# Sample attention on one Trainium2 core: pages turned on VectorE, scores in 32-row tiles, values undivided ahead of the next scores

## The reference, cut to what matters

```python
def mla_attend(q_lat, q_pe, q_pos, c_kv, k_pe, k_pos, w_uv):
    s = (jnp.einsum('bthc,bsc->bhts', q_lat, c_kv) + jnp.einsum('bthr,bsr->bhts', q_pe, k_pe)).astype(jnp.float32) * MLA_SCALE
    s = jnp.where(k_pos[None, :] <= q_pos[:, None], s, -jnp.inf)
    p = jax.nn.softmax(s, axis=-1).astype(c_kv.dtype)
    o_lat = jnp.einsum('bhts,bsc->bthc', p, c_kv)
    return jnp.einsum('bthc,chv->bthv', o_lat, w_uv)
...
    past = cache_mla[i][page_table].reshape(db, n_pages * PAGE_SIZE, MLA_LAT)
```

## Time and profile before

| | |
|---|---|
| median of 3 runs (lowest, highest) | 1845.02 us (1843.95, 1851.87) |
| span of the profiled execution, first to last instruction | 1837.3 us |
| profiled execution's own time | not given apart; the span and what lies around it, 7.7 us if it is the median |
| PE / DVE / ACT / POOL busy | 94% / 35% / 19% / 2% of the span |
| mean granted TensorE clock | 0.976 |
| prompt's attention with the first pair's pages | 126.4 to 181.7 us of the span |
| samples' attention, four pairs | 181.7 to 322.7 us |

### The profile page before, as it was taken

One profiled execution on the slowest core, in us unless ns is written; L12 is line 12 of the kernel. 1 busy time (PEld: TensorE's weight loads), 2 busy tenths in 40 slices (PEclk: granted clock), 3 DMA queues, 4 the chain that ended last, 5 costly groups with the idle time before them and its releaser, 6 DMA issues.

```text
span 1837.3 us, 41974 instructions
## 1 busy us (share of the span) xinstructions
PE 1732.0 (94%) x19056; PEld 1137.2 (62%) x19056; DVE 640.1 (35%) x1196; ACT 345.0 (19%) x558; POOL 39.7 (2%) x49
## 2 busy tenths in 40 slices
PE   6989898789899999998999999999999999999994
PEld 6967565589899999996934435344353534447342
DVE  5534443674865544855632010120101002010021
ACT  3223231402443333534210000000000000000001
POOL 0010000000000000000000000000000000010100
PEclk9999999698999999999999999999999999999998
DMA  9130540200854443517499999999999999997995
GB/s 292 52 112 1 150 141 20 38 3 4 240 161 151 150 137 105 170 62 230 172 386 414 418 413 418 415 417 417 410 417 403 417 415 406 417 398 306 415 405 220
DMA packets 171303, 474.02 MB, mean 258 GB/s; under 512 B 28426, under 2 KB 114604, under 8 KB 140228
## 3 DMA queue, kind: packets, MB, share of 16 engines
q1 hardware_dynamic: 168574, 461.05, 66.3%
q0 software_dynamic: 2352, 10.23, 1.6%
q10 hardware_dynamic: 198, 0.05, 0.0%
HBM read 459.19 MB, written 15.24 MB: 258 GB/s over the span
## 4 chain that ended last, share of the span: by engine, by line
PE 47%; SPq 3%; DMA 2%; DVE 1%; issue 1%; ACT 0%; POOL 0%; POOLq 0%; ACTq 0%; DVEq 0%
PE bank L2662 43%; SPq L2321 2%; DMA ring<-in_moe_w_down 1%; PE bank L319 1%; PE bank L320 1%; PE bank L321 1%; SPq L2431 0%; SPq L2325 0%; PE bank L2513 0%; PE bank L2592 0%; PE bank L2636 0%; DMA ring<-y_rows_dram,y_index 0%; PE bank L2528 0%; PE bank L2547 0%; PE bank L2630 0%
## 5 line engine op out<-in xcount | busy, mean ns | idle before, releaser
L2662 PE MATMUL bank<-ring,x 128*32 128x512 f32 (+1 forms) x6144 | 587.3, 540 | 2.3 <-DMA ring<-in_moe_w_gu 2.0
L2662 PEld LDWEIGHTS bank<-ring,x 128*32 128x32 f32 x6144 | 203.9, 110 | 354.4 <-issue 333.7
L2662 PE MATMUL bank<-ring,hid 128*32 128x256 f32 x5376 | 292.1, 379 | 0.3 <-DMA ring<-in_moe_w_down 0.3
L2662 PEld LDWEIGHTS bank<-ring,hid 128*32 128x32 f32 x5376 | 184.4, 110 | 108.1 <-issue 2.3
L319 PE MATMUL bank<-x_hi,w_hi 128*128 128x320 f32 (+1 forms) x488 | 151.8, 311 | 0.0
L320 PE MATMUL bank<-x_lo,w_hi 128*128 128x320 f32 (+1 forms) x488 | 150.8, 309 | 0.0
L321 PE MATMUL bank<-x_hi,w_lo 128*128 128x320 f32 (+1 forms) x488 | 150.8, 309 | 0.0
L2130 DVE TENSOR_TENSOR w_lo<-ring,w_hi 128x2048 fp32r<-128x2048 f32 (+2 forms) x51 | 112.5, 2209 | 97.5 <-ACT w_hi L2052 97.2
L3015 DVE TENSOR_TENSOR hrow<-sil,bank 128x512 f32<-128x512 f32 (+1 forms) x48 | 26.9, 617 | 301.3 <-PE bank L2662 301.3
L2052 ACT ACTIVATE w_hi<-ring 128x2048 fp32r<-128x2048 f32 (+2 forms) x51 | 94.1, 1848 | 126.8 <-PE bank L321 124.2
L2787 ACT ACTIVATE sil<-bank 128x512 f32<-128x512 f32 (+1 forms) x48 | 22.7, 544 | 455.2 <-PE bank L2662 455.2
(11 more groups left out here) (576 smaller groups left out, 2122.8 us busy)
## 6 DMA issues: line engine op xcount, KB each, us to landing
ring<-in_moe_w_gu SPq DMA_DIRECT2D x128, 1024.0 KB
ring<-in_moe_w_down SPq DMA_DIRECT2D x112, 1024.0 KB
ring<-in_moe_w_gu SPq DMA_DIRECT2D x128, 768.0 KB
ring<-in_ffn_w_gu_even SPq DMA_DIRECT2D x44, 512.0 KB, 4.9
pages<-in_cache_mla SPq DMA_DIRECT2D x128, 144.0 KB, 2.5
ring<-in_w_in_odd SPq DMA_DIRECT2D x12, 1024.0 KB, 5.3
ring<-in_ffn_w_down_even SPq DMA_DIRECT2D x10, 1024.0 KB, 5.4
proj_ring<-in_w_in_even SPq DMA_DIRECT2D x9, 1024.0 KB
```

Source lines behind the costliest of these rows:

```text
L2662: mm = t.matmul(ps[banks[g3]][SL * y:SL * y + SL, 0:w], act[:, g3, k, :], m_ring[:, slot, at + y * w:at + (y + 1) * w], start=start, stop= ...
```

## The change

**Turning pages.** PE's transposes and the copies out of PSUM are gone. DVE turns a page in 32x32 blocks from SBUF to SBUF: ten instructions for a pair (`QUARTERS`, four pages of 256 columns for one sample each, and two of 512 columns for the rotated keys). In such a block layout the latent's 32 rows of a chunk lie in each of the four groups of 32 partitions, one group for each quarter of a page's positions.

**Scores.** Nine chunks of 32 rows in place of three. For each chunk there are eight products: rows group k (32 partitions) by sample x (64 columns), `tile_position=(32*k, 64*x)`, 512 keys each, group k into bank k. The queries must lie in all four groups of partitions: SyncE writes them to DRAM once and loads them back for each pair (`load_queries`, four DMAs).

**Order.** `scores(p+1)` follows directly on the values of pair p. The values stay undivided in bank 4 or 5 (`acc(p)`), ACT divides them on the way out. ACT does all copies of turned probabilities and values. `mix` moves from DVE to POOL. SP loads quads 0 and 1 once half of the values that used the buffer are through (`v_half`), then waits for the scores of the pair before (`s_full`) to load the queries, then for `v_full` for the other quads.

```diff
+                def load_queries(sp, pair):
+                    for g in range(4):
+                        sp.dma_start(qrep[32 * g:32 * g + 32, :, :], q_dram[:, :, 2 * NQ * pair:2 * NQ * (pair + 1)].rearrange("c r q -> r c q")).then_inc(q_in, 16)
...
-                NT = 20
...
+                QUARTERS = [(quad, x) for quad in range(4) for x in range(2)]
+                NT = len(QUARTERS) + 2
+                def turn(v, pair, rows, e):
+                    quad, x = QUARTERS[e] if e < len(QUARTERS) else (3, e - len(QUARTERS))
+                    v.wait_ge(page_in[(2 * pair + x) % 4][quad], 64 * (pair // 2 + 1))
+                    if e < len(QUARTERS):
+                        four = slice(4 * quad, 4 * quad + 4)
+                        return v.transpose(pgT[:, x, four, :], rows[:, x, four, 0:KVR])
+                    return v.transpose(pgR[:, x, :, :], rows[:, x, :, KVR:LAT])
...
+                                sp.wait_ge(q_low, 2)
+                                for c in range(2):
+                                    sp.dma_start(q_dram[4 * c:4 * c + 4].rearrange("c r q -> (c r) q"), qsl[c].rearrange("p b q -> p (b q)")).then_inc(q_stored, 16)
+                                sp.wait_ge(q_turned, 2)
+                                sp.dma_start(q_dram[CB - 1], q_rope[:, :, :].rearrange("p b q -> p (b q)")).then_inc(q_stored, 16)
+                                sp.wait_ge(q_stored, 48)
+                                load_queries(sp, 0)
...
                                     for h in range(STEPS):
...
-                                    if 2 * h < NT:
-                                        turn(2 * h)
...
-                                    if 2 * h < NT:
-                                        e = 2 * h + 1
-                                        v.wait_ge(t0_full, e + 1)
-                                        v.tensor_copy(turn_dst(e), ps[7][0:turn_rows(e), :]).then_inc(t0_dve, 1)
+                                    if h < NT:
+                                        turn(v, 0, pages01, h)
...
                                 if p >= 2:
+                                    sp.wait_ge(v_half, p - 1)
+                                load_pages(sp, p, pairs[p % 2], rows)
+                                sp.wait_ge(s_full, 5 * p)
+                                load_queries(sp, p)
+                                if p >= 2:
                                     sp.wait_ge(v_full, p - 1)
...
+                                for c in range(CB):
+                                    for k in range(4):
+                                        rows = slice(32 * k, 32 * k + 32)
                                         for x in range(2):
+                                            keys = pgT[rows, x, :, 32 * c:32 * c + 32] if c < CB - 1 else pgR[rows, x, :, :]
+                                            mm = t.matmul(ps[k][64 * x:64 * x + 64, :].rearrange("p (n i) -> p n i", n=NPAGE), qrep[rows, c, NQ * x:NQ * x + NQ], keys,
+                                                          start=(c == 0), stop=(c == CB - 1), tile_position=(32 * k, 64 * x))
...
+                            scores(0)
                             for p in range(NPAIR):
                                 turn_probs(p)
+                                for quad in range(4):
+                                    values(p, quad)
+                                new_values(p)
+                                if p + 1 < NPAIR:
+                                    scores(p + 1)
                                 turn_out(p)
...
+                                for e in range(NT) if p + 1 < NPAIR else ():
+                                    turn(v, p + 1, pairs[(p + 1) % 2], e).then_inc(pg_turned, 1)
+                                    if e == 3:
+                                        v.wait_ge(ex_ready, p + 1)
+                                        dv(v, v.tensor_reduce(m1[:, 2:3], esum, AX_X, ALU.add))
+                                        v.reciprocal(rsum[:, p:p + 1], m1[:, 2:3]).then_inc(sum_ready, 1)
```

More of the change, by code:

```diff
@@ L790, in scores @@
                                     mm.then_inc(p_score, 1)
[L792 to L801, removed]
                                 def turn_probs(h):
@@ L985, in _ @@
+                            po(g, g.memset(shifted[:, :], 0.0))
                             for p in range(NPAIR):
                                 if p:
-                                    g.wait_ge(pt_full, p)
+                                    g.wait_ge(pt_full, 5 * p)
                                 g.memset(Prow[:, NPAGE * P:NPAGE * P + 64], 0.0).then_inc(zeroed, 1)
+                                if p == 0:
+                                    g.wait_ge(last_taken, 1)
+                                for c in range(4 * p, min(4 * p + 4, RT)):
+                                    mix(c)
@@ L1002, in scores @@
                             def scores(p):
+                                t.wait_ge(q_in, 64 * (p + 1))
                                 if p:
[L1005 to L1018 removed]
@@ new lines, in turn_probs, with values @@
+                                    mm = t.transpose(ps[n // 4][:, (n % 4) * P:(n % 4 + 1) * P], Prow[:, n * P:(n + 1) * P], C("ident"))
+                                    if n % 4 == 3:
+                                        mm.then_inc(pt_full, 1)
+                                t.transpose(ps[6][0:64, 384:512], Prow[:, NPAGE * P:NPAGE * P + 64], C("ident")).then_inc(pt_full, 1)
+                            def values(p, quad):
+                                t.wait_ge(pt_taken, 5 * p + quad + 1)
+                                if quad == 0 and p >= 2:
+                                    t.wait_ge(o_ready, p - 1)
+                                for n in range(4 * quad, 4 * quad + 4):
+                                    for x in range(2):
+                                        mm = t.matmul(acc(p)[64 * x:64 * x + 64, 0:KVR], pr[:, n, NQ * x:NQ * x + NQ], pairs[p % 2][:, x, n, 0:KVR],
+                                                      start=(n == 0), stop=False)
+                                if quad == 1:
+                                    mm.then_inc(v_half, 1)
@@ L1117, in _ @@
-                                dv(v, v.tensor_reduce(m1[:, 1:2], esum, AX_X, ALU.add))
-                                dv(v, v.reciprocal(m1[:, 2:3], m1[:, 1:2]))
-                                for e in range(9, 18) if more else []:
-                                    if TAKER[e] == "D":
-                                        take(p + 1, e)
-                                        mix(5 * p + (e - 10) // 2)
-                                        if e == 16 and 5 * p + 4 < RT:
-                                            mix(5 * p + 4)
```

237 lines of the change are left out of this document (73 added, 164 removed).

## The result

The median is 1818.3 us (1814.5 to 1822.6, four times) against 1845.0 us (1844.0 to 1851.9, four times) before. The medians stand as 0.9855 to 1; the ratio given with the measurement, taken over the fast runs of both kernels, is 0.9837, with a 95% interval of 0.9808 to 0.9866. Single executions of the kernel before, those beside the later experiments included, lie between 1837.4 and 1858.4 us, so a few us between two medians say little. The forecast was 1822 us, in a range of 1812 to 1836.

The account below looks back on a forecast made before the run. PE was taken to bound prompt and samples before, SyncE's queue the samples after. 13 us (prompt) plus 10.3 (samples) gave 23.3 us saved: 1845.0 to 1821.7, say 1822; whole range 1812 to 1836.

Parts of the forecast that it names:

- Prompt's stage: Prompt's attention: dropping PE's transposes and its wait before L674 saves 13 us, bounds 10 and 14.2.
- The 1.2 us given back to VectorE's pace: Prompt's first steps: DVE sets the pace before there are values, so 1.2 us of the 14.2 are not gained.
- Scores: Samples' scores: nine chunks of 0.86 us, all eight tiles at once, 7.7 us instead of 10.3.
- 11.0 us by the efficiency measured for packed tiles: Samples' scores: at 70% efficiency 11.0 us instead of 7.7, the whole 6 us longer; left out of the sum.
- the rivals of four and of two at a time: Samples' scores: four tiles at once, 15.4 us, total 1845 (twice the scores, chance 0.10); two, 30.9 us, total 1907 (0.07).
- Softmax gap: Between a pair's scores and its turned probabilities: 6.8 us after the change, 4.9 before, for DVE's maxima no longer hidden.
- Clock: PE resuming with scores after longer idle gaps: 1.5 us lost each time; turned probabilities 2.0 to 3.2 us.
- SyncE is the bound: Samples' stage: SyncE's queue needs 31.5 us a pair, PE's chain 26 to 27; end at 130.7 us, 10.3 saved.
- PE's slack: In front of each pair's scores: PE idle some 5 to 12 us, its chain taking 26 to 27 us.
- Moved for nothing: `mix` on POOL, 9 us for four a pair behind a memset with over 20 us of slack: no cost.
- Everything behind is untouched and starts earlier by the same.: All stages behind the samples' attention: they keep their time and start earlier by the 23.3 us saved.
- The median's distance from the span: Whole kernel: the median of the runs stands 7.7 us above the profiled span, carried over unchanged.

Follow-up runs that it names:

- e7: Changed kernel with the first pair's ten block transposes three steps later in the prompt's pipeline; 1815.3 us, one execution.
- e2: Changed kernel without the run-time bounds checks on the page numbers SyncE loads; 1801.0 us, ratio to the kernel before 0.9704 to 0.9821.
- e1: Changed kernel with the query DMAs from the second pair on issued by ACT instead of SyncE; 1814.3 us, ratio to the kernel before 0.9778 to 0.9897.
- e6: Changed kernel with the token shift's mixing back on DVE, POOL left with its memset; 1819.8 us, one execution.
- e5: Changed kernel in the old order, the next pair's scores behind turn_out; 1818.8 us, one execution.
- e10: Changed kernel without bounds checks, with query DMAs on ACT and the old order, scores behind turn_out; 1813.5 us, one execution.
- e9: Changed kernel without bounds checks, queries on ACT, 50 unread transposes in the softmax gap, most rotated keys turned early; 1792.7 us, ratio 0.966 to 0.9728.
- e11: Changed kernel without bounds checks, queries on ACT, 50 unread transposes in the softmax gap; 1793.4 us, ratio to the kernel before 0.9658 to 0.9719.
- e3: Changed kernel with 50 unread transposes on PE in the softmax gap; 1822.9 us, ratio to the kernel before 0.9797 to 0.9937.
- e8: Changed kernel without bounds checks and with the query DMAs on ACT; 1806.5 us, ratio to the kernel before 0.9735 to 0.9796.
- before_again: The kernel before, unchanged, run once more for a second trace; 1850.1 us, one execution.

## Why the prediction was right, step by step

- **Prompt's stage.** 14.0 us saved, 13 forecast. The 1.2 us given back to VectorE's pace was the error: the stage gained all but 0.2 of the 14.2 us taken from PE, and e7 shows that VectorE's first steps set nothing. The parts came out too: PE is busy 10.65 us less (49.37 to 38.72) for 10.2, and idle 3.35 us less (5.93 to 2.58) for 4.0. A block transpose takes 1.24 us, as worked out from an element's price; rotated parts 0.67 for 0.71.
- **Scores.** All eight tiles run at once: 0.86 us a chunk, 8.0 us in all for 7.7. The estimate from the Trainium skill ("TensorE: Matmul & The Clock Gate", Part 3), 11.0 us by the efficiency measured for packed tiles, isn't borne out here, and the rivals of four and of two at a time fall with it.
- **Softmax gap.** From the last chunk of scores to the turned probabilities 6.7 us (175.75 to 182.41), 6.8 forecast.
- **Clock.** 1.5 us forecast for scores that resume, 1.5 to 2.5 measured; turned probabilities 3.7 us, outside the 2.0 to 3.2 given (the row of 3.21 us behind it is of 16 transposes, not 17, and only part of it ran at the lower level).
- **SyncE is the bound.** Forecast 31.5 us a pair, measured 31.8 and 31.7; first distance 36.5 and 35.5; end of the stage 130.7 and 130.0 us from its start. Four query DMAs were mostly 1.9 us for 2.5, and the rest of a period 30.3 and 29.0 for 29.0 and 28.8, the second with 0.7 us of waiting. e2 shows the bound, since it takes only register work from the queue and each distance falls by 4.7 to 8.0 us; e1 agrees in the sum. What I had too large was PE's slack: with the low clock its chain took 29.3 us (203.22 to 232.5; scores 10.5, gap 6.7, probabilities 3.8, values 8.3) and not 26 to 27, so it stood 8.5 us ahead of the second scores but 2.5 and 3.4 us ahead of the later ones, not 5 to 12. The term that was too small is the low clock's.
- **Moved for nothing.** Right: e6 shows no price for `mix`, e5 none for the order while the queue is the bound; where PE is, the old order's 1.1 us stands in e10's rows.
- **"Everything behind is untouched and starts earlier by the same."** This step failed, and it was one of the prediction's own signs of being wrong: 3.9 us of the 25.0 saved up to the stage's end are given back in the RWKV block. In all fourteen profiles the clock falls between 0 and 3.2 us behind the stage's last copy. In five the lag was 45.4 to 46.7 us, and in each the low stretch that begins there lasts 13.7 us; in eight it was 48.2 to 49.9, with 27.3 to 30.7 us of low clock; in e1, with 17.1, it was 47.1. The 24 products shown above (L1398 before, L1340 after) took 4.52 us in just these eight and 2.50 to 2.57 in the other six. So the traces show that the block pays with the clock, though no edit varied it; what decides how long it stays low is open. Both profiles of the kernel before are among the five, with e9 and e11, which fill PE's gaps, and with e7, which does not; e3 fills them too and is among the eight. So neither the thinner stage nor its gaps explain it by themselves.
- **The median's distance from the span.** I carried 7.7 us over. After the change it is 2.1. The first profile of before was a favourable execution: its span is 1837.3 us, that of the second 1848.2, which is 1.9 us below its own time. So the 7.7 us were not what lies around the span but mostly the distance of a lucky profile from the median. The sum by the first profiles is 14.0 + 11.0 - 3.9 = 21.1 us, the medians differ by 26.7, and against the second profile of before it would be 32.0. Of the 3.4 us between 23.3 forecast and 26.7 measured, 1.7 are more gain up to the stage's end, -3.9 the loss behind it, and 5.6 the scatter in the carry. So part of the hit was luck: two errors of opposite sign.

## What to carry to other kernels

When work leaves the busiest engine, write the next queue's program out instruction by instruction, register reads included: here the issuing queue's 31.5 us a pair stood between a stage shorter by 11 us (141.0 to 130.0) and one shorter by 29 (to 111.6). Dropping its bounds checks gave 18 us of the stage, all the other edits on top of it 4; by the ratios to the kernel before it was about 14 and 12 us of the whole, and each of these ratios is uncertain by 5 to 11 us. They can be dropped only where the page numbers are known to be in range. Filling an idle TensorE to keep its clock pays only where TensorE is what the others wait for; under another bound the same instructions gained nothing. And don't count a gain in one stage as a gain of the whole before the block behind it is read: here it lost 3.9 us at the low clock in the profile of the change, for a reason that stays open.

## What the runs showed of the hardware

- Reading page numbers with bounds checks occupies SyncE's queue: without them, 32 page DMAs with the reads between them took 19.8 us instead of 27.4. The reads for eight pages alone took 0.85 us (204.37 to 205.22 in e2) instead of 2.89 (191.31 to 194.20 in after), so the checks 0.25 us a page.
- Eight tiles of 32 rows by 64 columns, float32 in two records each, took 0.86 us for 16 records of 512 columns, as long as two tiles took for four records.
- DMAs of 288 small pieces issued from ACT's queue between SyncE's page DMAs landed after up to 7.1 us in e8, and the pages issued beside them after 4.4 to 5.9 instead of 2.3 to 3.1; in e1 these pages landed after 3.9 to 5.8.
- TensorE's granted clock fell to its lower level, 0.50 of full (1.2 of 2.4 GHz), for 17 to 24 us around 125 to 149 us of the span, in three of fourteen profiles (before_again, e3, e10); PE was busy 95 to 100% of that time. Ten others have the full clock there, with the same program up to that point, and e11 a low stretch of 3.4 us ahead of it. What set it off, no run tells.
